# Square sums of three q or k tiles made together in three column blocks of TensorE, in one decoder layer on one core

## The reference

```python
def l2norm(x):
    return x * lax.rsqrt(jnp.sum(x * x, axis=-1, keepdims=True) + EPS)

qkv_a, gdn_conv_new = causal_dwconv(qkv_a, gdn_conv_prev, P['gdn_conv_w'][l])
qkv_a = jax.nn.silu(qkv_a.astype(f32))
qa, ka, va = [t.reshape(B, L, H_A, HEAD_DIM) for t in jnp.split(qkv_a, 3, axis=-1)]
...
oa, S_new = gated_delta_rule(l2norm(qa), l2norm(ka), va, beta, g, gdn_S0.astype(f32))
```

## Time and profile before

| | us |
|---|---|
| median of 3 runs | 1810.51 |
| their lowest and highest | 1808.78, 1812.75 |
| the profiled execution | 1808.62 |
| its span | 1806.8 |
| mean granted clock of the span | 0.925 |
| TensorE busy | 1588.7 (88%) |
| six norms' products (line 788), busy | 15.6 |

### The profile page before, as it was taken

How to read it: one execution, slowest core, us unless ns; L and a number is a source line. 1 busy time by engine, 2 the same in 40 slices (tenths; PEclk the granted TensorE clock), 3 DMA queues, 4 the chain that set the end, 5 groups by cost and what they waited for, 6 DMA issues and landing times. The chain is left out here.

```text
span 1806.8 us, 27711 instructions
## 1 busy us (share of the span) xinstructions
PE 1588.7 (88%) x10583; PEld 1393.2 (77%) x10587; DVE 1038.2 (57%) x1730; ACT 625.1 (35%) x1112; POOL 745.0 (41%) x837
## 2 busy tenths in 40 slices
PE   4689988999688877899699569999999999699996
PEld 2568887899566655689577469999999999588874
DVE  1561008650355534455334496887777776669885
ACT  2432132231244433122223334443433343444352
POOL 0541013221000005686103378999999996000011
PEclk7899999999899888789799888999999999799998
DMA  8335531230311128442132201222222222795862
GB/s 320 127 125 184 175 99 62 77 104 18 122 62 38 39 81 230 118 119 69 67 137 94 82 33 60 82 87 72 78 79 72 73 80 85 238 292 177 282 237 96
DMA packets 136981, 210.98 MB, mean 117 GB/s; under 512 B 38756, under 2 KB 78484, under 8 KB 133522
## 3 DMA queue, kind: packets, MB, share of 16 engines
q1 hardware_dynamic: 134386, 200.31, 33.9%
q10 hardware_dynamic: 2464, 8.91, 1.3%
HBM read 166.14 MB, written 42.91 MB: 116 GB/s over the span
## 5 line engine op out<-in xcount | busy, mean ns | idle before, releaser
L2696 DVE SCALAR_TENSOR_TENSOR fu_tmp<-fu_zp,fu_cw,fu_tmp 128x1024 f32<-128x1024 f32 x88 | 150.6, 1712 | 76.0 <-ACT fu_tmp L2631 74.4
L2441 PE MATMUL fu_ps<-fu_thi,fu_wlo 128*128 128x272 f32 (+2 forms) x672 | 139.1, 288 | 0.0
L2441 PE MATMUL fu_ps<-fu_thi,fu_whi 128*128 128x272 f32 (+2 forms) x672 | 138.9, 288 | 0.0
L2441 PE MATMUL fu_ps<-fu_tlo,fu_whi 128*128 128x272 f32 (+2 forms) x672 | 138.9, 288 | 0.0
L3018 PE MATMUL fd_ps<-fd_bhi,fd_ahi 128*128 128x512 f32 x308 | 121.3, 394 | 19.2 <-DVE fd_blo L3129 19.2
L2473 POOL TENSOR_TENSOR fu_wlo<-fu_s,fu_whi 128x512 fp32r<-128x512 f32 x84 | 119.4, 1432 | 18.9 <-ACT fu_whi L2587 18.3
L2587 ACT ACTIVATE fu_whi<-fu_s 128x512 fp32r<-128x512 f32 x84 | 50.9, 629 | 215.7 <-PE fu_ps L2441 89.4
L3018 PE MATMUL fd_ps<-fd_bhi,fd_alo 128*128 128x512 f32 x308 | 121.2, 393 | 0.0
L3018 PE MATMUL fd_ps<-fd_blo,fd_ahi 128*128 128x512 f32 x308 | 121.1, 393 | 0.0
L2441 PE MATMUL fu_ps<-h_hi,fu_whi 128*128 128x272 f32 (+1 forms) x504 | 105.6, 291 | 15.4 <-POOL fu_wlo L2473 15.4
L2473 POOL TENSOR_TENSOR fu_wlo<-w_raw,fu_whi 128x512 fp32r<-128x512 f32 x67 | 109.8, 1641 | 9.7 <-ACT fu_whi L2587 9.7
(11 more groups left out here) (398 smaller groups left out, 4040.1 us busy)
## 6 DMA issues: line engine op xcount, KB each, us to landing
wa<-in_w_ada SPq DMA_DIRECT2D x24, 1024.0 KB, 5.6
w_raw<-in_w_up SPq DMA_DIRECT2D x88, 256.0 KB, 2.5
fd_b<-in_w_down SPq DMA_DIRECT2D x86, 256.0 KB, 3.7
fd_a<-scr_y SPq DMA_DIRECT2D x86, 256.0 KB, 3.5
scr_y<-fu_tmp SPq DMA_DIRECT2D x22, 544.0 KB, 4.4
fp_w<-in_w_fm SPq DMA_DIRECT2D x15, 512.0 KB, 3.6
scr_qkv<-fp_y SPq DMA_DIRECT2D x9, 512.0 KB, 2.9
dr_stg<-scr_qkv SPq DMA_DIRECT2D x8, 576.0 KB, 6.0
```

The source lines that it names most:

```text
L2441: last = pe.matmul(lane_of(q, o)[:, n, 0:size], w[:, o, kk], part(low, kk, slice(c, c + size)), start=(kk == 0 and m == 0), stop=(kk == HK ...
L2696: one = dve.scalar_tensor_tensor(yp, a, w, yp, ALU.mult, ALU.add)
```

## The change

The squares of three tiles (all q, then all k) are kept in three slots of `sq`. TensorE makes no product for a = 0, 1, 3 and 4. For a = 2, in tile 5, and a = 5, in tile 8, it makes three products for each of the three pieces, one for each slot. The stationary matrix has 32 columns, of which the last 30 are zero, and product j writes partitions 32j to 32j + 31 of the bank. VectorE empties 96 partitions in one instruction, with the same factor for all of a group, after the convolution of a = 3 and of a = 6. SP copies the two rows of each block to `ln`, three transfers one behind the other, and waits for VectorE in tiles 5 and 8 alone. `ln` now lies in twelve rows of the tile `reset` that are otherwise unused. The table of constants is 30 columns wider. The squares on ScalarE are the same six, in the same order.

```diff
-C_COMB = C_HALF + 2
+C_COMB = C_HALF + 32
...
-        sq = sb("fp_sq", [P, TOK])
-        rb = sb("fp_r", [2, TOK])
-        ln = sb("fp_ln", [2 * H_A, TOK])
+        sq = sb("fp_sq", [P, PAIRS, TOK])
+        rb = sb("fp_r", [32 * PAIRS, TOK])
...
+        ln = reset[0:2 * H_A]
...
-                    if a < NQK:
-                        sp.wait_ge(r_set, 3 * a + 3)
-                        sp.dma_start(ln[2 * a:2 * a + 2], rb[:]).then_inc(r_out, 16)
+                    if a < NQK and a % PAIRS == PAIRS - 1:
+                        sp.wait_ge(r_set, a + 1)
+                        for j in range(PAIRS):
+                            h = 2 * (a + 1 - PAIRS + j)
+                            sp.dma_start(ln[h:h + 2], rb[32 * j:32 * j + 2]).then_inc(r_out, 16)
...
-            def norm(a, p):
+            def norm(g, p):
                 c, w = PIECES[p]
                 if p < 2:
-                    pe.wait_ge(sq_set, a + 1)
-                    after(pe, r_set, 3 * a)
+                    pe.wait_ge(sq_set, PAIRS * (g + 1))
+                    after(pe, r_set, 3 * g)
                 else:
-                    pe.wait_ge(r_set, 3 * a + 1)
-                pe.matmul(N_BANK[p][0:2, 0:w], K.cst[:, C_HALF:C_HALF + 2], sq[:, c:c + w], start=True, stop=True)\
-                    .then_inc(n_mm, 1)
+                    pe.wait_ge(r_set, 3 * g + 1)
+                for j in range(PAIRS):
+                    last = pe.matmul(N_BANK[p][32 * j:32 * j + 32, 0:w], K.cst[:, C_HALF:C_HALF + 32], sq[:, j, c:c + w],
+                                     start=True, stop=True)
+                last.then_inc(n_mm, 1)
...
                 a, t = i - 3, 2 * (i - 12)
+                g = a // PAIRS if 0 <= a < NQK and a % PAIRS == PAIRS - 1 else None
...
-                    if 0 <= a < NQK and kk == KD - 1:
-                        norm(a, 0)
-                        norm(a, 1)
+                    if g is not None and kk == KD - 1:
+                        norm(g, 0)
+                        norm(g, 1)
...
-                            pe.wait_ge(r_set, 3 * NQK)
+                            pe.wait_ge(r_set, NQK)
...
-                    if 0 <= a < NQK and kk == KD // 2:
-                        norm(a, 2)
+                    if g is not None and kk == KD // 2:
+                        norm(g, 2)
...
-                    after(act, n_mm, 3 * i)
-                    act.activation(sq[:], yb[:, i % 3], ACT.Square).then_inc(sq_set, 1)
+                    after(act, n_mm, 3 * (i // PAIRS))
+                    act.activation(sq[:, i % PAIRS], yb[:, i % 3], ACT.Square).then_inc(sq_set, 1)
...
-            def norm(a):
-                after(dve, r_out, 16 * a)
+            def norm(g):
+                after(dve, r_out, 16 * PAIRS * g)
                 for p, (c, w) in enumerate(PIECES):
-                    dve.wait_ge(n_mm, 3 * a + p + 1)
-                    dve.tensor_scalar(rb[:, c:c + w], N_BANK[p][0:2, 0:w], EPS, float(HD) if a < PAIRS else 1.0, ALU.add, ALU.mult)\
+                    dve.wait_ge(n_mm, 3 * g + p + 1)
+                    dve.tensor_scalar(rb[:, c:c + w], N_BANK[p][0:32 * PAIRS, 0:w], EPS, 1.0 if g else float(HD), ALU.add, ALU.mult)\
                         .then_inc(r_set, 1)
...
-                if 0 < i <= NQK:
-                    norm(i - 1)
+                if 0 < i <= NQK and i % PAIRS == 0:
+                    norm(i // PAIRS - 1)
```

## The result

| | before | changed |
|---|---|---|
| median, us | 1808.2 (10 runs) | 1792.59 (10 runs) |
| lowest and highest | 1801.59, 1812.75 | 1788.96, 1800.38 |
| profiled execution, us | 1808.62 | 1788.96 |
| its span, mean granted clock | 1806.8, 0.925 | 1787.1, 0.932 |

The ratio is 0.9933 with a 95% interval of 0.9918 to 0.9948, which is 12.1 us less (9.4 to 14.8). The medians differ by 15.6, so the gain is known to some microseconds and not to one. Before read 1810.51 over its first three runs and 1808.2 over ten. A second set of runs of the changed kernel gave 0.9924 (0.9906 to 0.9943), medians 1807.82 and 1793.65.

The account below looks back on a forecast made before the run. TensorE, busy throughout nearly every feature-stage tile, was taken as the bound. Gains of 7.47 and 7.19 less 0.40 and 1.0 gave 13.26 us, so 1810.51 - 13.3 = 1797.2 us, range 1794 to 1802.5.

Parts of the forecast that it names:

- Part 1: Feature stage, tile 3: first norm moves to tile 5, idle time ahead of tile 4 is 1.99 instead of 4.90, gaining 7.47 us.
- Part 2: Feature stage, tiles 4 to 8: six norms become two groups, plain tiles take 12.04 us, gaining 7.19 us.
- Part 3: Tiles 5 and 8: a group of three costs 0.20 us more than one norm, 0.40 in all (0.2 to 1.0).
- Part 4: Ahead of tile 4: 1.99 us idle may let the clock fall, costing 2.1 us; half taken, 1.0 us.
- Part 5: Feature stage: squares, evictions, row transfers and the wider constants on the other engines cost nothing.
- The sum: Whole kernel: 7.47 + 7.19 - 0.40 - 1.0 = 13.26 us gained.
- slower, by the layout: Rival: wider constants move every tile behind, slowing TensorE's streams everywhere; at 1.5% the time is 1821 us. Chance 0.04.
- One after another: Rival: a group's three column blocks don't overlap, costing 8.0 us in all; gain 5.6, time 1804.9. Chance 0.08.
- The late eviction: Rival: TensorE waits for VectorE's first eviction before the 64-column piece, up to 2.4 us a group; time 1802.0. Chance 0.07.
- Given back behind the stage: Rival: later stages lose the gain by other stretches at the lower clock; time about 1809 us. Chance 0.04.

Follow-up runs that it names:

- The filled idle time: Changed kernel with ScalarE rounding tile i + 3's weights ahead of the SiLU and SP loading tile 4's weights before waiting for decay rows: 1787.91 us, ratio 0.9898.
- The serial kernel: Changed kernel with each group's three products summed one behind the other into the same six partitions, without blocks of 32 columns: 1798.45 us, ratio 0.9951.
- 66 columns: Kernel before with a stationary matrix of 66 columns, 64 of them zero, in the six norms instead of 2 columns: 1802.93 us in one execution.
- the changed memory alone: Kernel before with only the changed kernel's memory: wider constants, three square slots (one used), high eviction tile, rows in reset: 1806.36 us, ratio 0.9996.

## Why the prediction was right

The time was 1792.59 us against 1797.2. The median lies 1.4 us under the range of 1794 to 1802.5; the ratio's 12.1 us of gain, with 9.4 to 14.8 around it, agrees with the 13.3 forecast, and puts the changed kernel at 1798.4 on the forecast's base of 1810.51. The base itself read 2.3 us lower over ten runs. So 13.3 lies between two readings of the same runs, 12.1 and 15.6, and that the whole comes this near is partly luck: the ten runs of the changed kernel spread over 11 us, and attention was shorter by 2.9 us in the profiles, which the forecast didn't have. The account rests on the feature stage, where each term can be read by itself.

- *The first norm (Part 1).* Idle time ahead of tile 4: 1.99 us forecast, 1.99 measured, released by ScalarE's high weights. Right in size and in what ends last. The filled idle time shows that nothing else waited behind it.
- *Six norms to two (Part 2).* Tiles 6 and 7 at 12.04 as forecast. Tile 4 took 12.16, 0.12 more, at its first products after the idle time.
- *The price of a group (Part 3).* +0.20 per group forecast, +0.10 measured (14.53 against 14.43). The serial kernel shows what it would have been without the overlap, +3.66; the forecast put that at 4.0.
- *The clock (Part 4).* The two rows on which the forecast rests were read wrongly in part. The lower clock ahead of 46.46 was no fall after 2.43 us of idle time; the clock had been low for 15 us before, with products running for 9.4 of them, as the window below this list shows. So neither row shows a fall brought by an idle time of 2 us. The forecast took half of 2.1 us. A fall costs 1.5: products run at the lower level for 3.4 us (298.2 to 301.6 in the second profile), where they did for 4.4 (294.4 to 298.8) in the first norm of before. It came in three of the changed kernel's four profiles: 1.1 on average against 1.0. That the mean came out so near is luck, with the price too high and the chance too low.
- *Nothing from the rest (Part 5).* Right: no wait on `fp_r` by TensorE in the changed kernel, no later wait on ScalarE's squares.
- *The sum.* Without a fall the forecast said 14.26 us for tiles 3 to 9; the profile without one has 14.34. With a fall it is 93.67 - 80.84 = 12.8.

The window of TensorE in the kernel before that belongs to the clock (Part 4), with its busy time, count and granted clock:

```profile
29.20:44.00 14.80, 9.44 (x40) 0.50 0.92 349
```

The Trainium skill's rule on draining, TensorEngine Tiling (Array Packing), Key Properties, was weighed wrongly. The prediction said that the trace shows none of it, since the product at 27.91 starts 0.07 us ahead of the end of the block before, 27.98. That reading can't show it, for the ends are modelled: the low products at 312.77 start 0.07 us ahead of the end of psR's, 312.84, in just the same way, and with 66 columns they start 0.50 us sooner. The 66 columns show 0.13 us a border in the mean, which agrees with the rule. The sum wasn't hurt, because the 2.40 us of a norm already held the four borders: its two columns lie within a block of 32 too, which the prediction didn't see. So of the 14.3 us, an estimated 4 x 0.52 = 2.1 are the sixteen borders of the four norms that are gone. As for the speedup of 2.38 for three column blocks in the Trainium skill, TensorE: Matmul & The Clock Gate, Measured speedup vs the span model, these rows show 2.8 to 2.9; the measurement decides.

The rival *slower, by the layout* is excluded by the changed memory alone. *One after another* is excluded by the rows of the group. *The late eviction* exists, at 0.12 us and only where a norm stands in tile 4. *Given back behind the stage* didn't happen: the profiled execution gained 5.3 us more than tiles 3 to 9 gave. The forecast doesn't explain that.

## What to carry to other kernels

Small products that use few output columns run side by side if each writes its own 32 partitions and they are issued together: three cost 1.04 to 1.01 times one here, between the starts of the 512-column pieces, on a path that is TensorE alone. Ask first what the first of them waits for: a third of this gain was a wait and a slow stretch, and what was left of the wait moved to the next step of ScalarE's order, where changing that order took away the rest (204.2 against 207.6 us of feature stage where the clock had fallen). A reader of a profile should look for blocks of columns that are used already; where there is just one product to make, filling it with zeros up to more than half the array was cheaper here by 0.52 us a norm. And before a gain in a stage that the change doesn't touch is counted, look at when the clock fell ahead of it.

## What the runs showed of the hardware

- Three fp32 products of 128 x 512 in three blocks of 32 columns took 0.89 us in psN and 0.96 in psR from start to start, one after another 2.58 and 2.67.
- Going from products over the whole array to products of 2 columns and back cost 0.13 us per border in the mean, 0.52 per norm, more than to products of 66 columns, between products of 128 x 364. The modelled ends of products don't show it.
- Behind 2 us of idle time the granted clock fell to its lower level in four of six profiles, and cost 1.5 us in the products that followed.
- A stage with the same 1330 records of TensorE took 180.9 to 185.1 us, with a granted clock of 0.92 to 0.90. In fourteen profiles the long ones are those in which the clock had fallen 3.11 to 3.72 us ahead of its first product. Why is open.
